# Two query blocks in one TensorE step for the paired heads of a 1,024-wide two-block transformer, and one copy moved ahead

## The reference, cut to what matters

```python
s = jnp.einsum('bqhmd,bkhmd->bhmqk', qblk, k) * scale      # differential attention, m = 0, 1
p = jax.nn.softmax(jnp.where(mask, s, -jnp.inf), axis=-1)
pd = p[:, :, 0] - lam * p[:, :, 1]
out = jnp.einsum('bhqk,bkhe->bqhe', pd, v)                  # then rmsnorm(out) * silu(z)
```

## Time and profile before

| | us |
|---|---|
| median of 3 executions | 2328.06 |
| lowest, highest | 2327.0, 2328.45 |
| the profiled execution, its own time | 2326.94 |
| its span, first to last instruction | 2325.2 |
| TensorE busy (matmuls) | 2311.6, 99% of the span |
| VectorE busy | 1478.5, 64% |
| ScalarE busy | 981.3, 42% |
| mean granted TensorE clock | 0.999 |

### The profile page before, as it was taken

One profiled execution on the slowest core, in us unless ns is written; L12 is line 12 of the kernel. 1 busy time (PEld: TensorE's weight loads), 2 busy tenths in 40 slices (PEclk: granted clock), 3 DMA queues, 4 the chain that ended last, 5 costly groups with the idle time before them and its releaser, 6 DMA issues.

```text
span 2325.2 us, 30164 instructions
## 1 busy us (share of the span) xinstructions
PE 2311.6 (99%) x11444; PEld 1880.9 (81%) x11444; DVE 1478.5 (64%) x2773; ACT 981.3 (42%) x1825; POOL 0.2 (0%) x4
## 2 busy tenths in 40 slices
PE   9999999999999999999999999999999999999998
PEld 7888888888888888888877788888887768888887
DVE  6788764345578774344577668566566767668565
ACT  5356542223446653222567533133236664323222
POOL 0000000000000000000000000000000000000000
PEclk9999999999999999999999999999999999999999
DMA  5333333332343333333221232314303112422322
GB/s 176 106 107 105 99 104 91 100 95 96 91 116 105 105 93 116 100 98 111 65 87 55 64 129 91 127 59 140 126 29 97 55 46 100 145 82 90 130 70 91
DMA packets 73583, 226.32 MB, mean 97 GB/s; under 512 B 14240, under 2 KB 15136, under 8 KB 72672
## 3 DMA queue, kind: packets, MB, share of 16 engines
q1 hardware_dynamic: 73296, 224.13, 30.9%
q10 hardware_dynamic: 144, 0.26, 0.0%
HBM read 204.83 MB, written 2.10 MB: 89 GB/s over the span
## 4 chain that ended last, share of the span: by engine, by line
PE 97%; DVE 1%; ACT 1%; DMA 0%; issue 0%; DVEq 0%; SPq 0%
PE bank L585 26%; PE bank L587 25%; PE bank L586 25%; PE bank L2196 2%; PE bank L2194 2%; PE bank L2195 2%; PE bank L1279 2%; PE bank L2009 1%; PE bank L1968 1%; PE bank L1266 1%; PE bank L1993 1%; PE bank L519 1%; PE bank L1256 1%; PE bank L1254 1%; PE bank L2022 1%; PE bank L2051 0%
## 5 line engine op out<-in xcount | busy, mean ns | idle before, releaser
L585 PE MATMUL bank<-h_hi,w_hi 128*128 128x512 f32 x1984 | 788.1, 397 | 0.7 <-DVE w_lo L1125 0.2
L587 PE MATMUL bank<-h_lo,w_hi 128*128 128x512 f32 x1984 | 774.0, 390 | 0.0
L586 PE MATMUL bank<-h_hi,w_lo 128*128 128x512 f32 x1984 | 773.7, 390 | 0.0
L585 PEld LDWEIGHTS bank<-h_hi,w_hi 128*128 128x128 f32 x1984 | 372.9, 188 | 83.1 <-issue 10.4
L1125 DVE TENSOR_TENSOR w_lo<-raw_w,w_hi 128x1024 fp32r<-128x1024 f32 x314 | 379.1, 1222 | 93.1 <-ACT w_hi L1113 89.9
L587 PEld LDWEIGHTS bank<-h_lo,w_hi 128*128 128x128 f32 x1984 | 372.5, 188 | 79.3
L586 PEld LDWEIGHTS bank<-h_hi,w_lo 128*128 128x128 f32 x1984 | 373.2, 188 | 72.7 <-issue 1.2
L1113 ACT ACTIVATE w_hi<-raw_w 128x1024 fp32r<-128x1024 f32 x314 | 327.7, 1054 | 145.5 <-DMA raw_w<-w_dram 145.2
L2429 ACT ACTIVATE nrm<-bank 128x512 f32<-128x512 f32 x44 | 26.4, 599 | 289.5 <-PE bank L587 289.5
L1568 ACT ACTIVATE ext<-bank 128x512 f32<-128x512 f32 x48 | 28.7, 599 | 279.7 <-PE bank L587 279.7
L1868 DVE TENSOR_TENSOR rope_a<-ext,bank 128x512 f32<-128x512 f32 x32 | 22.0, 688 | 160.9 <-PE bank L587 107.4
(11 more groups left out here) (369 smaller groups left out, 3506.4 us busy)
## 6 DMA issues: line engine op xcount, KB each, us to landing
raw_w<-w_dram SPq DMA_DIRECT2D x312, 512.0 KB, 3.6
down_raw<-w_dram SPq DMA_DIRECT2D x36, 512.0 KB, 4.4
extra_raw<-w_dram SPq DMA_DIRECT2D x10, 512.0 KB, 4.5
k_lo<-k_lo SPq DMA_DIRECT2D x32, 128.0 KB, 2.4
ln_row<-row_dram SPq DMA_DIRECT2D x4, 1024.0 KB, 6.8
last_raw<-w_dram SPq DMA_DIRECT2D x8, 512.0 KB, 4.5
x<-x_dram SPq DMA_DIRECT2D x4, 512.0 KB, 6.4
rowp<-row_dram SPq DMA_DIRECT2D x2, 1024.0 KB, 9.8
```

What stands on the lines that cost most here:

```text
L585: nc.tensor.matmul(dst, lh, rh, start=start, stop=False)
L586: nc.tensor.matmul(dst, ll, rh, start=False, stop=False)
L587: return nc.tensor.matmul(dst, lh, rl, start=False, stop=stop)
```

## The change: what it does

Block 1. For heads 4, 5 and 6 (`JOINED1`) the steps (a, 0) and (a, 1) become one group (`GROUPS1`). TensorE makes the scores of both blocks, the second in columns 128 to 383 of the same bank (`columns1`); then comes the work of the steps before, and both tiles' halves run one after the other. Later, the weighted sums of both blocks stand together, and so do their transposes. ScalarE copies both blocks' transposes with one instruction for each head of the pair. The late work is exchanged for all heads: value transposes in step (a, 2), the sum of squares in step (a, 3). On VectorE the epilogue of head a-2 now stands behind `normalise(a, 0)`, `split_squares` stands in step (a, 2), and the first part of the paired heads' epilogue in step (a, 2) where head a is joined. ScalarE's `output_squares` moves to step (a, 2) for head 4.

Block 2. The copy of the tile "kr" is issued before the two exponentials of its step.

```diff
-                LATE1[a, 3] = ("v", a + 1)
+                LATE1[a, 2] = ("v", a + 1)
             if 1 <= a <= N_A:
-                LATE1[a, 2] = ("sum", a - 1)
+                LATE1[a, 3] = ("sum", a - 1)
...
+        JOINED1 = range(N_A, LAST)
+        GROUPS1 = []
+        for a in range(N_ATT):
+            GROUPS1 += [((a, 0), (a, 1))] if a in JOINED1 else [((a, 0),), ((a, 1),)]
+            GROUPS1 += [((a, 2),), ((a, 3),)]
...
+        def columns1(a, qb):
+
+            return slice(P, 3 * P) if second1(a, qb) else slice(0, (qb + 1) * P)
...
+            for i, group in enumerate(GROUPS1):
+                a, qb = group[0]
+                if qb == 0 and a in (0, LAST):
+                    fill(a, qb, 0)
+                if banks1(a, qb) is S:
+                    for own in group:
+                        scores(*own)
+                if (a, qb) == (LAST, NB - 2):
+                    scores(a, qb + 1)
+                if qb or a not in (0, LAST):
+                    fill(a, qb, 0)
+                if i >= 2:
+                    for own in GROUPS1[i - 2]:
+                        pv(*own)
+                if i:
+                    for own in GROUPS1[i - 1]:
+                        transposes(*own)
+                fill(a, qb, 1)
+                late(a, qb)
+                for own in group[1:]:
+                    fill(*own, 0)
+                    fill(*own, 1)
+                    late(*own)
+                gate_early(NB * a + qb)
...
             def pT_copy(a, qb):
+                together = a >= N_A and a in JOINED1 and qb == 0
+                width = columns1(*last1(a, qb)).stop if together else (qb + 1) * P
...
-                    if qb == 1 and 1 <= a <= N_A:
+                    if qb == (2 if a in JOINED1 else 1) and 1 <= a <= N_A:
                         output_squares(a - 1)
...
-                    if qb == 0 and 2 <= a < N_A + 2:
-                        epilogue(a - 2)
-                    elif qb == 1 and a > N_A:
+                    if qb == (2 if a in JOINED1 else 1) and a > N_A:
                         epilogue(a - 1, False)
                     elif qb == 3 and a > N_A:
                         split_y(8 + a - 1 - N_A)
                         dve.wait_ge(y_ready, at(y_ready, 4 + a))
                     normalise(a, qb)
-                    if qb == 1 and 1 <= a <= N_A:
+                    if qb == 0 and 2 <= a < N_A + 2:
+                        epilogue(a - 2)
+                    if qb == 2 and 1 <= a <= N_A:
                         split_squares(a - 1)
...
+                if "kr" in ENDS[step, 0]:
+                    tile_copy("kr")
                 if is_sb(step):
                     sb_softplus(a, qb)
...
-                    tiles_out([name for name in ENDS[step, 0] if name not in ("uk0", "uv0")])
+                    tiles_out([name for name in ENDS[step, 0] if name not in ("kr", "uk0", "uv0")])
```

More of the change, by code:

```diff
@@ L1250, in scores @@
                         pe.wait_ge(tile_out[t], at(tile_out[t], before1(B1_GATE)))
+                own = columns1(a, qb)
                 for m in range(2):
-                    if u and bank is S:
+                    if u and bank is S and not second1(a, qb):
                         pe.wait_ge(max_ready, at(max_ready, u - 1 + m))
-                    nc.tensor.matmul(bank[m][:, 0:nk], q_two[i][m][:, block_q], k_two[i][m][:, 0:nk], start=True, stop=False)
+                    nc.tensor.matmul(bank[m][:, own], q_two[i][m][:, block_q], k_two[i][m][:, 0:nk], start=True, stop=False)
                 for m in range(2):
-                    nc.tensor.matmul(bank[m][:, 0:nk], q_two[i][m][:, block_q], k_lo[i][m][:, 0:nk], start=False, stop=True) \
+                    nc.tensor.matmul(bank[m][:, own], q_two[i][m][:, block_q], k_lo[i][m][:, 0:nk], start=False, stop=True) \
                       .then_inc(scores_ready, 1)
@@ L1261, in transposes @@
                 for m in range(1 if a < N_A else 2):
-                    i = ti1(a, qb, m)
-                    if i >= 2:
+                    i, own = ti1(a, qb, m), columns1(a, qb)
+                    to = own.start if a >= N_A else 0
+                    if i >= 2 and not (a >= N_A and second1(a, qb)):
                         pe.wait_ge(t_out, at(t_out, i - 1))
                     for b in range(qb + 1):
-                        last = nc.tensor.transpose(T[i % 2][:, b * P:(b + 1) * P], pn[m][:, b * P:(b + 1) * P], ident)
+                        last = nc.tensor.transpose(T[i % 2][:, to + b * P:to + (b + 1) * P],
+                                                   pn[m][:, own.start + b * P:own.start + (b + 1) * P], ident)
                     last.then_inc(t_ready, 1)
@@ L1323, in tensor_block1, with late @@
                 tile1(n, 1)
[L1325 to L1345, removed]
+            def late(a, qb):
+                use, f = LATE1.get((a, qb), (None, 0))
+                if use == "v":
+                    v_transpose(f)
+                elif use == "sum":
+                    sum_squares(f)
+            for i, group in enumerate(GROUPS1):
[22 more added lines that the diff above has]
+                gate_early(NB * a + qb)
             pv(LAST, NB - 2)
@@ L1550, in scalar_block1 @@
                     softmax_exp(a, qb, 1)
+                    if before and not second1(a, qb):
+                        for own in GROUPS1[GROUP1_AT[a, qb] - 1]:
+                            if not (own[0] >= N_A and second1(*own)):
+                                pT_copy(*own)
                     if before:
-                        pT_copy(*before)
                         if LATE1.get(before, ("", 0))[0] == "sum":
                             output_rstd(LATE1[before][1])
-                    if qb == 1 and 1 <= a <= N_A:
+                    if qb == (2 if a in JOINED1 else 1) and 1 <= a <= N_A:
                         output_squares(a - 1)
@@ L1789, in normalise @@
             def normalise(a, qb):
-                nk = (qb + 1) * P
+                own = columns1(a, qb)
                 l, r = small[:, 32 + 2 * qb:34 + 2 * qb], small[:, 40:42]
```

39 lines of the change are left out of this document (23 added, 16 removed).

## The result

| | before | after |
|---|---|---|
| median, us | 2327.11 (19 executions) | 2331.69 (19 executions) |
| lowest to highest | 2326.34 to 2328.45 | 2330.65 to 2332.38 |
| the profiled execution, its span | 2326.94, 2325.2 | 2331.44, 2329.6 |
| mean granted TensorE clock | 0.999 | 0.999 |

The ratio is 1.0020, interval 1.0014 to 1.0026: 4.6 us slower, forecast 3.7 slower. That is 0.197%, at the edge of the 0.2% which the prediction took as the least that a measurement can tell, and its interval lies on both sides of that edge.

The account below looks back on a forecast made before the run. TensorE was taken as the bound (97% of the last chain). Joins -2.3, late sum of squares +6.7, block 2 -0.7 gave +3.7 us: 2331.8 us from 2328.06, eight-in-ten range 2326.0 to 2338.0.

Parts of the forecast that it names:

- Bound, and what can count: Whole kernel: the last chain lies 97% on TensorE, so only what alters TensorE's work or makes it wait counts.
- What joining removes: Block 1, heads 4 to 6 of two layers: one break of the tile stream less per group, 6 x 0.38 = 2.3 us less.
- The remainder of step (5, 2): Block 1, paired step: 0.38 of 7.19 us left after its counted work, taken as the cost of breaking off the tile stream.
- The moved sum of squares: Block 1, heads 2 to 5: late root delays epilogue and normalising, TensorE waits; 3.3 us per layer, 6.7 us in all.
- 0.54, 0.43, 0.74 and 0.66: TensorE's forecast waits for probabilities, us: the first two in each of heads 2 and 3, then head 4, head 5.
- later than VectorE by my count: Block 1, joined heads 4 and 5: the next transposes follow two blocks' sums, so TensorE was to have no second wait.
- E: Block 1: the end of the transposes T(a-1,3), from which the lateness of root, epilogue and probabilities is counted.
- Two loads of 1.28 us: ScalarE's root in block 1: logarithm and exponential each load a table, making it 3.83 us; no drain of 1.38 us added.
- Block 2, 0.7 us: Block 2: rotary key copy 1.35 us sooner removes TensorE's 0.35 us wait at the maximum per layer; bounds 0 and 0.7.
- 1: Rival: VectorE is in time and only the gain stays, 2325.1 us; one way is one table for both functions; chance 0.12.
- 2: Rival: later query rotation holds up SyncE's queue, weight loads come late and ScalarE's casts wait; 2340 us, chance 0.15.
- 3: Rival: the joined groups' score banks become the wait, slack 0.2 us; 4 x 0.3 us, 2333 us; chance 0.05.

Follow-up runs that it names:

- experiment 8: Changed kernel with the reciprocal root issued ahead of ScalarE's copy of the transposed probabilities and no joined heads; 2325.74 us, ratio 0.9994 to the kernel before.
- experiment 9: Changed kernel with the reciprocal root ahead of the copy of the transposed probabilities, and heads 1 to 3 joined too; 2323.84 us, ratio 0.9985 to the kernel before.
- experiment 3: Changed kernel with the old order, row sum in the third step, in the unjoined heads 1 to 3; 2325.19 us, ratio 0.9993 to the kernel before.
- experiment 5: Changed kernel with block 1's reciprocal root ahead of ScalarE's copy of the transposed probabilities; 2323.55 us, ratio 0.9985 to the kernel before.
- experiment 6: Changed kernel with Exp in place of Ln in block 1's reciprocal root (values wrong, prices the table loads); 2323.97 us, ratio 0.9986 to the kernel before.
- experiment 7: Changed kernel with the Ln of block 1's reciprocal root made twice, root 0.6 us longer; 2336.85 us, ratio 1.0041 to the kernel before.
- experiment 10: Changed kernel with the reciprocal root ahead of the copy and the row sum of heads 1 to 3 back in the third step; 2323.42 us, ratio 0.9985.
- experiment 2: Changed kernel with no joined heads, its other edits kept; 2331.12 us, ratio 1.0018 to the kernel before.

## Why the prediction was right, and where its sizes were off

The mechanism held; that the sum of its terms came within 0.9 us of the measured difference is in part luck, since the lateness was 1.7 us too small and block 2's gain 1.1 us too small.

- **Bound, and what can count.** Right: everything that moved the time moved TensorE, by waits at transposes, by starts of paired sums and by one bank in block 2.
- **What joining removes, 2.3 us.** Right in size (experiment 8: 2.05), wrong in what it was called. The remainder of step (5, 2) is a property of paired steps (experiment 9); carried over to unpaired ones it misled me in experiment 9.
- **The moved sum of squares, 6.7 us.** The mechanism was right in every link (experiments 3, 5, 6 and 7 each cut or stretched one link), the size too small. Block 1 lost 6.1 net, so with 2.3 for the joins 8.4 were lost. The waits themselves read 0.60, 0.50, 0.93 and 0.70 for 0.54, 0.43, 0.74 and 0.66. Three terms are missing in the sum. Each head of two waits took about 0.1 us more than its two rows of waiting (1.2 against 1.10). The joined head 5 waited a second time, where the prediction had said "later than VectorE by my count"; of that row's 0.26 us, 0.17 are the ordinary change behind paired sums, which the kernel of experiment 5 has at the same place, so 0.09 was waiting:

```profile
275.89 0.64 PEld L1287 LDWEIGHTS bank<-const,pn 128*128 128x128 f32 x6 [0.17 <-issue]
```

  And heads 0 and 1 took 0.12 and 0.15 more in the two layers. This stays with the root first (experiments 5, 8 and 9) and goes with the row sum early (experiments 3 and 10), so it belongs to the exchange of the late work; which instruction makes it is open. The prediction's own working has a slip as well: E + 13.69 and 7.89 us make E + 21.58, not 21.61, so its second wait is 0.40 and its sum 6.6.

  In head 4 the probabilities came at E + 13.39 (E is 226.79 + 0.60 now, the last `normalise` ends at 240.78), forecast 13.31; the rest of that miss is TensorE's, which was ready some 0.15 us earlier than its forecast E + 12.67. What the sum got wrong in kind is the split between its terms: it books 0.38 of gain for the join and 0.74 of loss for the late sum in head 4, but experiment 2 shows that without the join the late sum costs nothing there.
- **Two loads of 1.28 us.** Right, and without them nothing waits (experiment 6): their 2.56 us is more than each of TensorE's waits. The drain that the Trainium skill ("ScalarE: Activation LUTs", What ACT_TABLE_LOAD costs) adds is not in the profile after either: the load from 169.62 ends at 170.90, the exponential starts at 170.92. On the same page, Table sets gives one load for a logarithm followed by an exponential; the changed kernel has two in each of eight heads, the kernel of experiment 6, with exponentials alone, has none there.
- **Block 2, 0.7 us.** Too small; the step that failed is "I take that wait away once in each layer". That row held 0.35 us of ordinary start and 0.2 of waiting, the latter in one layer only. What the edit gave besides was 0.79 in each layer, beyond the stated bounds of 0 and 0.7 for both, at a stall that I had not looked for: the copy's own bank. I followed what the copy feeds and not what it frees, and the row of the stall named VectorE.
- **Rivals.** 1: no, for the reason given against it, the two loads. 2: its signs are there, its cost isn't. SyncE's longest wait for the query's rotation rose from 2.5 to 4.0 us, and ScalarE's casts do wait for loads more often (the rows below: SyncE after, then ScalarE before and after). In block 1's attention, from head 1 on, they wait 11 times in each layer, 14 and 15 us in all, where it was 3 times, 2.5 and 3.3 us. That was a sign by which the forecast "would be wrong". But TensorE's waits for split weights stayed as they were (1.9 us in three times in both kernels, none of them in this attention), and experiment 5 still has 17 such waits of ScalarE, up to 2.5 us, without a wait of TensorE at the probabilities. So these waits stopped at ScalarE; whether the loads came later or ScalarE came sooner to them stays open. 3: no wait at the joined groups' score banks; experiment 7 shows how near it was.

```profile
SPq L1017 <- DVE q_lo L1812: 42.1, 14, 4.0
```

```profile
ACT w_hi L1113 <- DMA raw_w<-w_dram: 145.2, 66, 4.5
```

```profile
ACT w_hi L1132 <- DMA raw_w<-w_dram: 167.7, 83, 4.8
```

- **The signs to look for.** Found: the twelve waits, 0.48 to 0.93 us, VectorE idle 3.6 to 3.9 us before the epilogue, stretches of 36 tile matmuls. The last sign, "block 2's wait at the fused maximum gone", came only in the second layer and in name.

## What to carry to other kernels

When work is moved behind an instruction that waits for another engine, it takes over that wait. Look at the idle time that the queue has just in front of the moved piece: here ScalarE stood 1.0 to 2.8 us for a copy while its next task had its input ready, and exchanging the two turned a loss of 4.6 us into a gain of 3.3 against the kernel before. And for a copy out of a bank, ask what it frees as well as what it feeds: the releaser that a row names can be one that happened to end at about the same time.

## What the runs showed of the hardware that was not expected

TensorE's weight loader stands in most places where products of full size (128*128) and products that use half the rows or half the columns (64*128, 128*64) follow one another, in both directions. In the trace this appears as a wait for "issue", or for whatever engine happened to finish then. From full to half size it is 0.35 us behind a product of 512 columns (24 times 8.5 us at block 1's paired sums in the kernel before) and 0.17 us behind one of 128 columns; from half size back to full it is 0.17 us behind paired sums of 128 columns (30 times 5.1 us), and in block 2 it is 0.33, 0.54 and 0.76 us behind half-row products of 256, 384 and 512 columns; behind those of 128 columns there is none. Unpaired sums, of full size behind full size, have no such row. The kernel before, weight loader, step (5, 2), then block 2, behind 128 columns of full size, and behind 384 and 512 columns of half the rows:

```profile
268.72 0.20 PEld L1279 LDWEIGHTS bank<-pT,vs 128*64 128x64 f32 x4 [0.35 <-issue]
269.09 0.42 PEld L1266 LDWEIGHTS bank<-const,pn 128*128 128x128 f32 x4 [0.17 <-issue]
...
1201.06 0.30 PEld L1968 LDWEIGHTS bank<-ks,qs 64*128 64x128 f32 x4 [0.17 <-issue]
...
1294.44 0.30 PEld L1974 LDWEIGHTS bank<-cum_r,sel_r 128*128 128x128 f32 x2 [0.54 <-issue]
...
1300.62 0.30 PEld L1974 LDWEIGHTS bank<-cum_r,sel_r 128*128 128x128 f32 x2 [0.76 <-issue]
```

A logarithm and an exponential in turn bring a table load of 1.28 us each, sixteen loads in the profile of the changed kernel's attention; with exponentials alone (experiment 6) these sixteen are gone.
